# Gate-up weights in rows 264 columns apart, and another order of the passes in the third block

## The reference

```python
hn = rms_norm(h, norm2_g)                                   # block one
gate, up = jnp.split(hn @ w_gate_up, 2, axis=-1)
h = h + (jax.nn.silu(gate) * up) @ w_down

x = x + 0.5 * swiglu(rms_norm_2(x, ffn1_norm), ffn1_w_gate, ffn1_w_up, ffn1_w_down)   # block two
...                                                         # two attentions, gates, output projection
x = x + 0.5 * swiglu(rms_norm_2(x, ffn2_norm), ffn2_w_gate, ffn2_w_up, ffn2_w_down)   # block three

def swiglu(h, w_gate, w_up, w_down):
    return (jax.nn.silu(h @ w_gate) * (h @ w_up)) @ w_down
```

## Time and profile before

| | |
|---|---|
| median of 2 runs | 2000.55 us (2000.34 to 2000.75) |
| the profiled execution, from first to last instruction | 1998.1 us |
| TensorE busy, matmuls | 1990.9 us, 9505 |
| TensorE, weight loads (overlap the matmuls) | 1668.7 us |
| GpSimd (POOL) busy | 1007.5 us |
| VectorE (DVE) busy | 877.9 us |
| ScalarE (ACT) busy | 732.3 us |
| DMA | 188.81 MB, 94 GB/s |

### The profile page before, as it was taken

One profiled execution on the slowest core, in us unless ns is written; L12 is line 12 of the kernel. 1 busy time (PEld: TensorE's weight loads), 2 busy tenths in 40 slices (PEclk: granted clock), 3 DMA queues, 4 the chain that ended last, 5 costly groups with the idle time before them and its releaser, 6 DMA issues.

```text
span 1998.1 us, 26696 instructions
## 1 busy us (share of the span) xinstructions
PE 1990.9 (100%) x9505; PEld 1668.7 (84%) x9505; DVE 877.9 (44%) x1467; ACT 732.3 (37%) x1034; POOL 1007.5 (50%) x795
## 2 busy tenths in 40 slices
PE   9999999999999999999999999999999999999999
PEld 8998887788888888888888888889888888888887
DVE  6587756535333322153334115677645523332124
ACT  6413234444222323232232225667643422322232
POOL 5444442245555544455555446565654555555443
PEclk9999999999999999999999999999999999999999
DMA  5233231133333332333332232332222333332332
GB/s 179 87 92 99 85 104 43 49 100 93 96 105 86 103 100 80 109 90 105 85 104 90 98 107 85 109 103 75 72 87 85 104 105 84 105 95 89 98 107 85
DMA packets 253787, 188.81 MB, mean 94 GB/s; under 512 B 6608, under 2 KB 249680, under 8 KB 253680
## 3 DMA queue, kind: packets, MB, share of 16 engines
q1 hardware_dynamic: 253024, 187.53, 31.5%
q10 hardware_dynamic: 688, 0.31, 0.1%
HBM read 180.93 MB, written 2.10 MB: 92 GB/s over the span
## 4 chain that ended last, share of the span: by engine, by line
PE 98%; ACT 1%; DVE 1%; issue 0%; DMA 0%; SPq 0%; ACTq 0%; DVEq 0%
PE ps L693 30%; PE ps L695 30%; PE ps L694 30%; PE ps L989 1%; PE ps L1141 1%; PE ps L1061 1%; PE ps L1062 1%; PE ps L1063 1%; PE ps L1129 1%; PE ps L1128 0%; PE ps L983 0%; PE ps L1111 0%; PE ps L1099 0%; PE ps L882 0%; PE ps L1098 0%
## 5 line engine op out<-in xcount | busy, mean ns | idle before, releaser
L566 POOL TENSOR_TENSOR wlo<-raw,whi 128x512 fp32r<-128x512 f32 (+2 forms) x636 | 852.9, 1373 | 862.1 <-ACT whi L1206 773.1
L693 PE MATMUL ps<-xh,whi 128*128 128x512 f32 (+1 forms) x1872 | 716.1, 383 | 0.0
L695 PE MATMUL ps<-xh,wlo 128*128 128x512 f32 (+1 forms) x1872 | 709.0, 379 | 0.0
L694 PE MATMUL ps<-xl,whi 128*128 128x512 f32 (+1 forms) x1872 | 708.7, 379 | 0.0
L1206 ACT ACTIVATE whi<-raw 128x2048 fp32r<-128x2048 f32 (+1 forms) x149 | 280.1, 1880 | 765.0 <-PE ps L695 764.9
L695 PEld LDWEIGHTS ps<-xh,wlo 128*128 128x128 f32 x1872 | 351.5, 188 | 66.8
L693 PEld LDWEIGHTS ps<-xh,whi 128*128 128x128 f32 x1872 | 351.7, 188 | 64.4 <-issue 0.7
L694 PEld LDWEIGHTS ps<-xl,whi 128*128 128x128 f32 x1872 | 352.0, 188 | 62.1 <-issue 0.7
L1736 DVE TENSOR_TENSOR tmp<-ps,rs 128x512 f32<-128x512 f32 x148 | 101.9, 691 | 313.1 <-PE ps L695 295.6
L695 PE MATMUL ps<-fh,wlo 128*128 128x512 f32 x528 | 205.4, 389 | 0.0
L693 PE MATMUL ps<-fh,whi 128*128 128x512 f32 x528 | 205.4, 389 | 0.0
(11 more groups left out here) (335 smaller groups left out, 2247.1 us busy)
## 6 DMA issues: line engine op xcount, KB each, us to landing
raw<-in_w_in SPq DMA_DIRECT2D x87, 512.0 KB, 4.6
raw<-in_w_gate_up SPq DMA_DIRECT2D x44, 512.0 KB, 4.7
raw<-in_ffn_w_gate SPq DMA_DIRECT2D x44, 512.0 KB, 4.0
raw<-in_ffn_w_up SPq DMA_DIRECT2D x44, 512.0 KB, 5.2
raw<-in_ffn_w_down SPq DMA_DIRECT2D x32, 512.0 KB, 4.0
raw<-in_w_down SPq DMA_DIRECT2D x16, 512.0 KB, 4.0
raw<-in_ffn_w_down SPq DMA_DIRECT2D x16, 384.0 KB, 3.6
raw<-in_w_b SPq DMA_DIRECT2D x8, 512.0 KB, 4.0
```

The source lines that it names most:

```text
L566: ins = pool.tensor_tensor(wlo[:, c % 2, cs], raw[:, c % 2, cs], whi[:, c % 2, cs].bitcast(F32), ALU.subtract)
L693: pe.matmul(o, w_of(whi), xhi, start=first, stop=False)
L694: pe.matmul(o, w_of(whi), xlo, start=False, stop=False)
L695: return pe.matmul(o, w_of(wlo), xhi, start=False, stop=last)
```

## The change

The gate-up chunks of all three blocks get rows 264 columns (`CP`) apart instead of 256; the 8 rows of a chunk so begin 0, 32, 64 ... 224 bytes further in a 256-byte line. A slot grows from 2048 to 2112 columns (`SLOT`), in all three buffers, and the default of `n_cols` with it, so that ACT's copy and POOL's subtractions take 2112 columns in every chunk that used the default. All other chunks keep rows of 256 columns. The 64 columns that those don't load are set to zero once at the start. All buffers behind `raw` move up by 512, 1024 or 1536 bytes. In the third block's gate-up stage the three passes run in another order: high weights with high activations, low weights with high activations, high weights with low activations.

```diff
+CP = 2048 // 8 + 8
+SLOT = 8 * CP
...
-        wide = [sb("raw", [P, EXT + 2 * CH]), sb("whi", [P, EXT + 2 * CH], F32R), sb("wlo", [P, EXT + 2 * CH], F32R)]
-        raw, whi, wlo = (w[:, EXT:EXT + 2 * CH].rearrange("p (s n) -> p s n", s=2) for w in wide)
+        wide = [sb("raw", [P, EXT + 2 * SLOT]), sb("whi", [P, EXT + 2 * SLOT], F32R), sb("wlo", [P, EXT + 2 * SLOT], F32R)]
+        raw, whi, wlo = (w[:, EXT:EXT + 2 * SLOT].rearrange("p (s n) -> p s n", s=2) for w in wide)
...
-            return CH
+            return SLOT
...
                         c = C_F[f] + j
-                        s = slot(c, DK, CW)
+                        s = slot(c, DK, CP)
                         sel = bass.ds(sp.snap(i * CW + P * j), P)
                         load(c, [(s[:, :, 0:P], gate[:, :, sel]), (s[:, :, P:CW], up[:, :, sel])], 2, i)
...
+            def passes_high_first(o, s, w_of, xhi, xlo, first, last):
+
+                pe.matmul(o, w_of(whi), xhi, start=first, stop=False)
+                pe.matmul(o, w_of(wlo), xhi, start=False, stop=False)
+                return pe.matmul(o, w_of(whi), xlo, start=False, stop=last)
...
-            def chunk(c, hi, lo, per=0, i=None, X=None, full=(False, False), widths=(P, P), between=None, steps=None, ready=None):
+            def chunk(c, hi, lo, per=0, i=None, X=None, full=(False, False), widths=(P, P), between=None, steps=None, ready=None, row=None, ordered=passes):
...
-                        w_of = lambda wt: wt[:, s, w * k + o0:w * k + o0 + m]
+                        w_of = lambda wt: wt[:, s, (row or w) * k + o0:(row or w) * k + o0 + m]
...
-                            mm = passes(ps[0:m, b, :], s, w_of, hi[:, k, cs], lo[:, k, cs], k == 0, k == DK - 1)
+                            mm = ordered(ps[0:m, b, :], s, w_of, hi[:, k, cs], lo[:, k, cs], k == 0, k == DK - 1)
...
-                chunk(c, xh, xl, X=X, between=(lambda: norm_sums(S, c)) if S == 2 else None,
+                how = dict(row=CP, ordered=passes_high_first if f == 2 else passes)
+
+                chunk(c, xh, xl, X=X, **how, between=(lambda: norm_sums(S, c)) if S == 2 else None,
                       steps=None if S == 2 else lambda t, k: norm_sums(S, c) if (t, k) == SUMS_AT else None)
-                chunk(c + 1, xh, xl)
+                chunk(c + 1, xh, xl, **how)
                 with pe.Fori(0, FK // 2 - 1) as i:
                     for j in range(2):
-                        chunk(c + 2 + j, xh, xl, 2, i)
+                        chunk(c + 2 + j, xh, xl, 2, i, **how)
...
             dve.memset(stk[:].bitcast(F32), 0.0).then_inc(stk_zero, 1)
+            dve.memset(raw[:, :, CH:SLOT], 0.0)
             dve.memset(ctok[:, QB, :], 0.0).then_inc(ctok_zero, 1)
```

## The result

The changed kernel takes 2016.6 us (2016.34 to 2016.86, 2 runs) against 2000.55 before: 1.008 times as long, 95% interval 1.0051 to 1.0109. It is 16 us slower, outside the range of 1988 to 2005 and on the other side of the forecast. It lies within the 2% that were given 0.96.

What follows compares the result with a forecast made beforehand. The prediction took the pace of TensorE's matmuls as the bound. Its terms, -6.5 us for the row distance, +1.6 for the larger slot and 0 for the rest, sum to -4.9: from 2000.55 to 1995.6 us, range 1988 to 2005.

Steps and rivals of the forecast that it cites:

- The bound: Whole kernel: TensorE is busy 1990.9 of 1998.1 us, so only its matmul pace or a new wait moves the end.
- Does the place show: Projections in the earlier trace: extra per matmul 13.1 to 13.3 ns where rows lie alike, 10.9 to 11.6 where not.
- part 1: Gate-up rows 264 columns apart: 3168 matmuls each save 1.7 to 2.4 ns, 6.5 us gained.
- Part 2: Slot larger by 64 columns: longer copies and subtractions make eight chunks about 0.2 us late each, 1.6 us lost.
- Parts 3, 4 and 5: Transfers landing elsewhere, passes exchanged in block three's gate-up, and the memset of 128 columns on DVE: 0 us each.
- Rival B: Gate-up pace gets worse by 1 to 5.7 ns in 3168 matmuls: 3 to 18 us, 2005 to 2020 us; chance 0.15.
- Rival A: Gate-up pace does not change, the extra not depending on addresses; only the larger slot's cost is left, 2002.2 us; chance 0.33.
- Rival C: Most of the gate-up extra goes: 6 to 13.3 ns per matmul, 19 to 42 us, 1960 to 1983 us; chance 0.10.

Runs made afterwards that it cites:

- Experiment 7: Kernel before, with both halves of the 264-column projections reading the same in-line columns of xh and xl; 1999.28 us against 2000.53.
- experiment 6: Kernel before, with only the order of the passes exchanged in block three's gate-up; 2000.24 us against 2000.13, ratio 0.9999.
- experiment 3: Kernel before, with 32 bytes of padding ahead of xh, moving xh, xl and all three weight buffers together; 2017.85 us against 2000.02.
- experiment 1: Three variants of the changed kernel: rows 256 columns apart, chunks moved by constant shifts, old pass order; 2020.2, 2017.4 and 2017.3 us against 2000.0, 2000.0 and 2000.1.
- experiment 5: Kernel before, block three's passes exchanged, with wlo alone, then xl alone, moved by 32 bytes; 2046.2 and 2025.2 us against 2000.1.

## Why the prediction was wrong

**The bound** was right: TensorE's pace is the time, and 15.0 of the 17.0 us lie in the steps of the gate-up matmuls.

**Does the place show** failed, and with it part 1. The step was "So the extra is 13.1 to 13.3 where all rows lie alike and 10.9 to 11.6 where they don't", used as a price for matmuls of 512 columns. The two groups with the low extra were also those of 264 columns; the text noted that no row separates the two and took the value all the same. Experiment 7 separates them: at 264 columns 10.0 ns in line and 11.7 out of line, and at 512 columns 13.3 and 18.1 (231.4 - 213.3). So lying out of line costs at both lengths, where the prediction took a saving of 1.7 to 2.4 ns: the term had the wrong sign, and not only the wrong size. The unevenness of the steps in the earlier trace rows did show that place matters, and a step of 0.13 us among steps of 0.12 was a cost, not a part of a gain. A comparison of like with like within the trace would have been row 0 of that projection, in line, with its seven others. By the start times its three steps sum to 356 ns and those of the others to 357 to 371, 364 in the mean: out of line costs some 2.5 ns per matmul there too, in six of the seven rows.

**The size** of part 1: 3168 x (231.4 - 226.65) = 15.0 us lost, instead of 6.5 gained; the three stages show 5.03 + 4.94 + 5.03 = 15.0.

**Part 2** met the sum, 1.6 forecast and 1.57 between the medians (whose interval is -0.2 to 3.6 us), but not in its places, so that the agreement is partly luck. Three chunks of the first down stage are late by 0.17 us in their first step and lose another 0.12 to 0.15 in the following ones, 0.91 in all instead of 0.6; at the merge and the second output projection it is 0.31 instead of 0.8; the last chunk of the w_b projection, whose late start of 0.14 us I had put down to POOL, is not late in the changed kernel at all, and in the kernel before the profile names no releaser for that wait, so POOL was not shown to cause it; and the 0.36 us after block two, mostly TensorE's wait for ACT at the first attention, was not foreseen. The hand-over needs no more than 0.05 us (762.68 + 5.17 = 767.85 to 767.90), not 0.24. The chunk of the earlier trace rows so had 0.19 us to spare and still came late by 0.17: beside the 0.06 of the copy and the 0.13 of the subtractions, its copy began 0.19 us later, counted from TensorE's start on the chunk before (765.33 - 761.52 = 3.81 us in the changed kernel, 759.79 - 756.17 = 3.62 before). ACT came to it later behind work that waits for DVE; what delayed that chain was not tested.

**Parts 3, 4 and 5** held: no wait of ACT for a DMA in gate-up, the order of the passes worth nothing (experiment 6), and behind the memset DVE still waits 0.43 us for the vectors (0.59 before).

**Rival B** is what happened, and inside its bounds (3 to 18 us, 2005 to 2020): 4.7 ns in 3168 matmuls, plus part 2. It had 0.15. Its own words, "decides against the change as soon as the mean extra rises at all", hold. Rival A and the rule behind it fall: the Trainium skill, "TensorE: Matmul & The Clock Gate", section "Step-by-step: what each phase is for", has the weight load take nothing from the running matmul. Here the load keeps its 188 ns, and the matmul over it pays 4.1 to 7.5 ns of 512 columns at fifteen of the nineteen distances, while with both moved together (experiment 3) nothing more than the 226.7 is seen. Rival C has nothing for it; of nineteen distances none is below 226.6.

## What to carry to other kernels

Where TensorE is the bound and float32r weights are loaded under a streaming operand, start both at the same offset in a 256-byte line, for every pair that is in flight together: that was the fastest place of all that were tried, and padding the rows to spread them over the line cost 4.7 ns per matmul. Other types than float32r were not run. A price for one length of matmul must not be taken from another length; look for the pair of rows that differs in one thing only, and if the trace has none, give the two signs the same chance. Padding a buffer is paid by all who copy it whole, and where a hand-over has 0.2 us to spare, work that ends 0.4 us later shows.

## What the runs showed of the hardware

- The step of a 512-column float32r matmul depends on the distance between the weights being loaded and the operand that streams, inside a 256-byte line: 226.7 ns at 0, 252 and 240 bytes (226.8), 228.8 at 192, 230.7 to 234.2 at fifteen others; moving both by 32 bytes changes nothing (experiments 1 and 3). The period is 256 bytes: in the kernel before, the rows of `xh` are 2304 bytes apart and those of the weights 1024, so that they lie at many multiples of 256 from each other, all at 226.7, while 128 bytes cost 5.7 ns.
- The distance is not all: at the same distances one tile (244 bytes, 226.7 for 233.2) and one block (`xl` moved, 231.1 for 233.3) ran faster than the rest.
- The weight load's record is 188 ns in line and out of line; the record of the matmul that streams over it goes from 389 ns to 392 to 398 (experiment 1, 32 and 64 bytes).
- One misplaced pair in three can be as dear as three: 233.3 ns on average in both (experiments 1 and 5, but for one block). The mean of three steps comes out at 233.3, that is 6.67 ns over the 226.7, for seven of the distances. Why this value, and why 192 bytes is cheaper, was not found.
- Where all pairs are in line, the steps of the five lengths tried that are multiples of 8 fit multiples of 6.67 ns: 120 ns for both 256 and 264 columns, 220.0 for 496, 226.7 for both 504 and 512. What makes the 10 to 17 ns on top of the columns stays open.
- The halves of the 264-column projections would be 1.7 ns faster in line, 576 of them, 1.0 us in all, if their tokens could be split so that both halves start in line. That wasn't tried; it is less than the spread of the runs of the kernel before (1999.7 to 2001.1 us). No version that computes the same and is faster than the kernel before was found.
